# The dilated stage's first two turns and its masks made between the last products of layer 1's pairs

## What is computed

```python
def band_attend(q, k, v, d, nw):      # per residue mod d, 128-query blocks
    s = einsum('bthe,bmhe->...', q, [previous block, own block] of k)
    s = where(valid, s, NEG)          # the masks
    p = exp(s - max(s)); l = sum(p)
    return (p / l) @ v, m + log(l)

def dil_layer(x, ...):
    z = rms_norm(x, norm_g) @ w_in    # projections; norm on q and k rows
    dil_out = combine of the three groups * silu(gd)
    mem_out = mem_attend(q, mem_kv) * silu(mg)
    return x + concatenate([dil_out, mem_out]) @ w_out
```

## Time and profile before

| | us |
|---|---|
| median of three executions | 2821.64 (2819.12 to 2824.57) |
| the profiled execution, its own time | 2820.37 |
| its span | 2818.2 |
| PE busy | 2759.3 (98%) |
| DVE, ACT, POOL busy | 1758.5, 1113.7, 364.9 |
| the pairs' last product | 2286.39 to 2289.11 |
| the sample rows' matmuls ahead of it | 2284.53 to 2286.39 |
| the masks on POOL | from 2294.99, a memset of 0.44 and three selects of 0.78 together |
| the dilated stage | 2289.11 to about 2512 |

### The profile page before, as it was taken

One profiled execution on the slowest core, in us unless ns is written; L12 is line 12 of the kernel. 1 busy time (PEld: TensorE's weight loads), 2 busy tenths in 40 slices (PEclk: granted clock), 3 DMA queues, 4 the chain that ended last, 5 costly groups with the idle time before them and its releaser, 6 DMA issues.

```text
span 2818.2 us, 38685 instructions
## 1 busy us (share of the span) xinstructions
PE 2759.3 (98%) x13662; PEld 2278.4 (81%) x13662; DVE 1758.5 (62%) x3819; ACT 1113.7 (40%) x3357; POOL 364.9 (13%) x574
## 2 busy tenths in 40 slices
PE   7999999999999999999999999999999989989999
PEld 6787888888787888888787888788888779988887
DVE  5486666768678633325575767776765656557664
ACT  5433131222326224215434453532323348756532
POOL 0001010100101000000001132313324022210000
PEclk9999999999999999999999999999999999999999
DMA  4276555555676634324266676868777788647642
GB/s 169 86 239 199 190 186 175 183 181 176 199 244 205 202 106 145 99 99 150 94 250 229 224 245 226 286 219 286 262 267 246 253 283 286 215 151 244 200 142 95
DMA packets 282873, 559.16 MB, mean 198 GB/s; under 512 B 31168, under 2 KB 81920, under 8 KB 282680
## 3 DMA queue, kind: packets, MB, share of 16 engines
q1 hardware_dynamic: 248440, 453.89, 49.5%
q0 software_dynamic: 34240, 102.80, 10.0%
HBM read 423.85 MB, written 132.72 MB: 197 GB/s over the span
## 4 chain that ended last, share of the span: by engine, by line
PE 93%; DVE 3%; DMA 2%; ACT 1%; issue 1%; SPq 0%; DVEq 0%; ACTq 0%
PE ps L130 26%; PE ps L132 25%; PE ps L131 25%; PE ps L3560 2%; PE ps L3532 2%; PE ps L3081 2%; PE ps L3065 1%; PE ps L3569 1%; PE ps L3119 1%; PE ps L237 1%; PE ps L2122 1%; PE ps L2390 1%; PE ps L3548 1%; PE ps L3543 1%; DMA tok_b_dram<-shared_o 1%; PE ps L1149 1%
## 5 line engine op out<-in xcount | busy, mean ns | idle before, releaser
L130 PE MATMUL ps<-b_wp,b_sring 128*128 128x512 f32 x640 | 250.3, 391 | 4.4 <-DMA b_sring<-sums_dram 3.7
L131 PE MATMUL ps<-b_wp,b_sring 128*128 128x512 f32 x640 | 249.8, 390 | 0.0
L132 PE MATMUL ps<-b_wp,b_sring 128*128 128x512 f32 x640 | 249.7, 390 | 0.0
L130 PE MATMUL ps<-a_sring,a_wp 128*128 128x512 f32 x512 | 199.5, 390 | 2.6 <-DMA a_sring<-sums_a_dram 2.6
L132 PE MATMUL ps<-a_sring,a_wp 128*128 128x512 f32 x512 | 199.3, 389 | 0.0
L131 PE MATMUL ps<-a_sring,a_wp 128*128 128x512 f32 x512 | 199.2, 389 | 0.0
L132 PE MATMUL ps<-b_wp,b_xtlo 128*128 128x512 f32 x480 | 186.8, 389 | 0.0
L131 PE MATMUL ps<-b_wp,b_xthi 128*128 128x512 f32 x480 | 186.8, 389 | 0.0
L130 PE MATMUL ps<-b_wp,b_xthi 128*128 128x512 f32 x480 | 186.8, 389 | 0.0
L960 DVE TENSOR_TENSOR shared_o<-ps,b_spare 128x512 f32<-128x512 f32 x160 | 109.7, 685 | 100.5 <-PE ps L132 83.1
L802 ACT ACTIVATE ps<-shared_o 128x128 f32<-128x128 f32 (+1 forms) x408 | 108.0, 265 | 154.7 <-DVE shared_o L960 146.9
(11 more groups left out here) (461 smaller groups left out, 6823.5 us busy)
## 6 DMA issues: line engine op xcount, KB each, us to landing
b_sring<-sums_dram SPq DMA_DIRECT2D x160, 512.0 KB, 5.1
a_sring<-sums_a_dram SPq DMA_DIRECT2D x128, 512.0 KB, 5.0
b_raws<-w_b_dram SPq DMA_DIRECT2D x176, 256.0 KB, 4.3
a_raws<-w_a_dram SPq DMA_DIRECT2D x140, 256.0 KB, 4.4
kv_dram<-shared_o POOLq DMA_DIRECT2D x96, 256.0 KB, 4.2
tok_b_dram<-shared_o POOLq DMA_DIRECT2D x96, 256.0 KB, 4.5
front<-tok_b_dram SPq DMA_DIRECT2D x96, 256.0 KB, 3.7
front<-grp_dram SPq DMA_DIRECT2D x48, 260.0 KB, 4.3
```

The costliest lines, as they stand in the source:

```text
L130: pe.matmul(acc, a_hi, b_hi, start=first, stop=False)
L131: pe.matmul(acc, a_hi, b_lo, start=False, stop=False)
L132: return pe.matmul(acc, a_lo, b_hi, start=False, stop=last)
```

## The change

A new class `Opening` holds the stage's first tiles and its buffers, and its methods are called from both stages.

- PE turns tile 0 ahead of product `N - 4`, the memory keys ahead of `N - 3` and tile 1 ahead of `N - 2`. These turns use banks 6 and 7. ACT and DVE make their copies at the same `n`, ahead of what they do for that product.
- POOL builds the masks at `n = N - 8`, ahead of the stores that follow.
- The sample rows' matmuls in phase 6 stand ahead of the product before the last, and their finish stands ahead of the last output's, in every pair.
- DVE no longer waits for the stores. SP loads tiles 0 to 3's queries and keys and the memory keys, then the values of tile 0, waits for the last product, and loads the values of tiles 1 to 3. Behind tile 4's queries and keys it waits for the stores of all outputs, then loads values 4 and all that follows.
- ACT runs one exponential on a column of `ident` at the start of the stage. The stage's loop on PE starts with round 2.
- The buffers lie elsewhere: values in three pieces (`dil_v0`, `dil_v1`, `dil_v4`).

```diff
@@ shared_stage
+    SAMPLED = {0: TP - 3, 1: TP - 1, 5: TP - 1, 6: TP - 2}
...
-        if r == 0 and j:
-            return sample_out(j - 1, 1), 5, 2 * j - 1
+        if r == PN - 2 and j < len(pairs):
+            return sample_out(j, 1), 5, 2 * j + 1
...
@@ POOL
             for n in range(N + 2):
                 j, f, p = where(n)
+                if n == N - TP:
+                    pool.wait_ge(keys.reduced, keys.UNITS)
+                    opening.build_masks(pool)
@@ ACT
+                if n == N - 4:
+                    opening.copy_query(act, 0)
+                if n == N - 3:
+                    for m in range(MT):
+                        opening.memory_high(act, m)
+                if n == N - 2:
+                    opening.copy_query(act, 1)
+                if n and sample_at(n - 1):
+                    evict(sample_at(n - 1)[0], sample_at(n - 1)[1])
...
-                if n and sample_at(n - 1):
-                    evict(sample_at(n - 1)[0], sample_at(n - 1)[1])
@@ DVE
-                at_once = n < N and out_of(n) is not None and kinds[out_of(n)] == "copy"
+                at_once = n == N - 1 or n < N and out_of(n) is not None and kinds[out_of(n)] == "copy"
+                if n == N - 4:
+                    opening.copy_keys(dve, 0)
+                if n == N - 3:
+                    for m in range(MT):
+                        opening.memory_low(dve, m)
+                if n == N - 2:
+                    opening.copy_keys(dve, 1)
@@ PE
-                if p == (TP - 1 if f else TP - 3) and f in (0, 1, 5, 6):
+                if f in SAMPLED and p == SAMPLED[f]:
                     sample(j, f)
+                if n == N - 4:
+                    opening.turn(pe, 0)
+                if n == N - 3:
+                    opening.turn_memory(pe)
+                if n == N - 2:
+                    opening.turn(pe, 1)
                 product(n)
@@ class Opening
+    def query_bank(self, s):
+        return self.core.ps[:, 0 if s > 1 else 6, :]
+    def turn(self, pe, s):
+        u, ident = s % self.U, self.core.ident
+        pe.wait_ge(self.qk_in[u], 32 * (s // self.U + 1))
+        if s == 1:
+            pe.wait_ge(self.mem_low, MT)
+        if s:
+            pe.wait_ge(self.q_copied, s)
...
@@ dil_stage, SP
             for sem, count in tail.stored(tail.projected):
                 sp.wait_ge(sem, count)
-            sp.wait_ge(*tail.made)
+            sp.wait_ge(*tail.made(0))
             sp.wait_ge(*tail.split)
             sp.wait_ge(*tail.weights)
+            sp.wait_ge(*tail.keys)
+            opening.load(sp, 0)
+            opening.load_memory(sp)
+            for s in range(1, U):
+                opening.load(sp, s)
+            load_values(0)
+            sp.wait_ge(*tail.made(NT // 2))
+            for s in range(1, U):
+                load_values(s)
+            for s in range(U, TILES):
+                opening.load(sp, s)
+                if s == U:
                     for sem, count in tail.stored(tail.outputs[1]):
                         sp.wait_ge(sem, count)
+                load_values(s)
...
@@ dil_stage, ACT, DVE and PE
+            act.activation(front.stat[:, 0, 0:1], ident[:, 0:1], ACT.Exp)
...
-            dve.wait_ge(masked, 3)
-            for sem, count in tail.stored(tail.outputs[1]):
-                dve.wait_ge(sem, count)
+            dve.wait_ge(opening.masked, 3)
...
-            for s in range(TILES + 2):
-                if s == 0:
-                    pe.wait_ge(*tail.bank_free(0))
+            for s in range(2, TILES + 2):
                 if s == 2:
-                    pe.wait_ge(*tail.outputs)
+                    for bank in range(3):
+                        pe.wait_ge(*tail.bank_free(bank))
...
                 if s == 3:
-                    pe.wait_ge(mem_low, MT)
+                    pe.wait_ge(*tail.outputs)
```

More of the change, by code:

```diff
@@ L503, in __init__, with shared_stage @@
         self.wh1, self.wl1 = prep.buffers(stack)
-def shared_stage(core, block, lead, prep, first, pairs, ops, bufs, xt_hi, xt_lo, xs_hl, spare, w_out, keys):
+def shared_stage(core, block, stack, lead, prep, first, pairs, ops, bufs, xt_hi, xt_lo, xs_hl, spare, w_out, keys, opening):
     nc, ps, io = core.nc, core.ps, core.io
@@ L3215, in out_stage, with dil_stage @@
                     stored=lambda t: (y_out[t % 2], 16 * (t // 2 + 1)) if t < NT else (dec.y_out, 16))
-def dil_stage(core, block, tail, q_src, kv_src, dst, front, ahead, mem_kv, ops_out):
+def dil_stage(core, block, tail, opening, dst, ahead, mem_v, ops_out):
     nc, ps, ident = core.nc, core.ps, core.ident
-    U, V, R = 4, 8, 3
+    front, place, rows = opening.front, opening.place, opening.rows
+    U, V, R = opening.U, opening.V, opening.R
     GROUPS = len(DIL)
     TILES = NT * GROUPS
[L3227 to L3234, removed]
+    kv_src, dst = opening.kv_src, dst[::-1]
@@ L3343, in _ @@
         def _(pool):
-            pool.wait_ge(*tail.keys)
-            pool.memset(masks[:, :], 0.0).then_inc(zeroed, 1)
-            pool.wait_ge(zeroed, 1)
-            for at, sign in ((0, -1), (1, 1), (2, -1)):
-                cols = masks[:, at * P:(at + 1) * P]
-                pool.affine_select(out=cols, in_=cols, compare_op=ALU.is_ge, fill=NEG, base=0,
-                                   pattern=[[-sign, P]], channel_multiplier=sign).then_inc(masked, 1)
             for s in range(TILES):
@@ L3397, in _ @@
                     exps(s - 2, 1)
-                if real(s):
-                    copy_query(s)
-                if s == 2:
-                    for m in range(MT):
-                        memory_high(m)
+                if s > 2 and real(s):
+                    opening.copy_query(act, s)
             act.wait_ge(front.qturned, 1)
@@ L3504, in _ @@
                     minima(s - 2, 1)
-                if real(s):
-                    copy_keys(s)
-                if s == 2:
-                    for m in range(MT):
-                        memory_low(m)
+                if s >= 2 and real(s):
+                    opening.copy_keys(dve, s)
             next_groups_max()
@@ L3559, in sums @@
                     for i, key in enumerate(order(s)):
-                        m = pe.matmul(sums_at(s)[:, h, :], pt[:, h, i, :], v_b[:, key % V, cols], start=(i == 0),
+                        m = pe.matmul(sums_at(s)[:, h, :], pt[:, h, i, :], v_at[key % V][:, cols], start=(i == 0),
                                       stop=(i == len(order(s)) - 1))
@@ L3656, in build @@
             keys.scores(st)
+            with ExitStack() as early:
+                opening = Opening(core, early, [io["tok_b"][g][0:T, :] for g in range(len(DIL))],
+                                  [io["kv"][g][0:T, :] for g in range(len(DIL))], mem_kv(1, 0), ops)
             with ExitStack() as ws:
@@ L3677, in build @@
                          Pair(gate(4), gate(5), norm_b)]
-                tail = shared_stage(core, block, lead, prep, (key(0), value(0)), pairs, ops, bufs, xt_hi, xt_lo, xs_hl,
-                                    spare, io["w_out_b"], keys)
-            front = Front(core, st)
-            dil_stage(core, block, tail, [io["tok_b"][g][0:T, :] for g in range(len(DIL))],
-                      [io["kv"][g][0:T, :] for g in range(len(DIL))],
-                      [io["grp"][g * T:(g + 1) * T, :] for g in range(len(DIL))], front, src,
-                      (mem_kv(1, 0), mem_kv(1, 1)), ops)
+                tail = shared_stage(core, block, st, lead, prep, (key(0), value(0)), pairs, ops, bufs, xt_hi, xt_lo, xs_hl,
+                                    spare, io["w_out_b"], keys, opening)
+            front = opening.front
+            front.open(core, st)
+            core.sb(st, "front_held", [P, 10800])
+            dil_stage(core, block, tail, opening, [io["grp"][g * T:(g + 1) * T, :] for g in range(len(DIL))], src,
+                      mem_kv(1, 1), ops)
             out_stage(core, block, 1, src, io["x1"][0:T, :], io["y"][0:T, :], ops, io["x1"][T:TS, :], io["y"][T:TS, :],
```

188 lines of the change are left out of this document (109 added, 79 removed).

## The result

The changed kernel takes 2825.35 us (median of 20 runs, 2820.73 to 2828.11), the kernel before 2821.4 (20 runs, 2816.57 to 2824.57). The ratio is 1.0013, with a 95% interval of 1.0007 to 1.0019: about 3.9 us more, slower beyond doubt and still within the 0.2% that the prediction counts as no change. The forecast was +5.2. The profiled execution of the changed kernel took 2826.09 (span 2824.2), 5.7 more than that of before.

What follows compares the result with a forecast made beforehand. PE was taken to be busy nearly throughout, with waits at the dilated stage's start. A gain of 5.3 us (22.85 - 2.6 - 14.9) against 10.6 for tile 0's wait and its clock gave +5.2 us, 2826.8, range +2.5 to +8.

Steps and rivals of the forecast that it cites:

- Where the time goes: PE before tile 0's turn, ahead of the last four products: a 7.7 us wait for a load issued 1.1 us late.
- The memory keys: Landing at the latest 2287.7 to 2288.6, with PE coming to them about 2290: load hidden, no wait.
- The last product's end: End of the last product before the dilated stage: 2289.11 + 2.6 moved work + 7.7 wait + 2.9 clock = 2302.3.
- The clock's 2.9: PE at half speed behind the wait for tile 0: 2.9 us lost.
- Behind the last product: From the last product's end to tile 5's turn: 14.9 us, set by tile 5's late load, where 22.85 stood before.
- The clock there: Between last product and tile 5: waits may lower PE's clock, 1.5 us more, covered by tile 5's late load.
- The end: Whole kernel: +5.2 us, 2826.8, from tile 5's start moving from 2311.96 to 2317.2.
- the forecast's own signs of being wrong: Tile 0 coming without a wait, the clock staying at full, or the tiles behind tile 5 waiting too.
- Rival A: At tile 0's turn: the tile lands fast, wait 4.1 and clock 1.6; -0.2 us, 2821.4; chance 0.22.
- B: At tiles 5 and 6: loads pile up, tile 6 waits about 1.5 more; +8.3 us, 2829.9; chance 0.13.
- C: At tile 0's turn: PE doesn't wait, the load being issued before 2273; -5.3 us, 2816.3; chance 0.05.
- D: Nothing on the whole: a hidden stall at the other pairs' ends takes or gives a microsecond or two; chance 0.05.

Runs made afterwards that it cites:

- the filler: The changed kernel with sixty transposes of the identity, read by nobody, in front of tile 0's turn: 2821.59 us, and 2822.9 when run again.
- the tile 5 edits: Tile 5's queries and keys loaded ahead of the wait for the stores: 2815.6 us with three loads early, 2824.45 on the changed kernel alone.
- the three early loads: The changed kernel with the loads of tile 0, the memory keys and tile 1 each issued behind an earlier ring load: 2814.28 us.
- tile 0's loads early: The changed kernel with only tile 0's queries and keys loaded some 8 us earlier, memory keys and tile 1 left in place: 2820.85 us.

## Why the prediction was right, and where not

- **Where the time goes: right.** A wait of 7.7 us in front of tile 0's turn was forecast, 7.62 and 7.36 came. It comes from SP's order (keys asked for 1.02 us after PE is ready, 1.1 forecast) and from the landing (6.55; 6.6 forecast). The Trainium skill (DMA: Bandwidth & Descriptors, section "Anatomy of one DMA — SWDGE (gpsimd) path") has the fit of 2.0 us plus the bytes over 436e3, 2.6 us here as an estimate; it was measured on transfers issued in another way than SP's, and no run here has such a load alone. This one took 3.9 more, at a DMA share of 0.90 (2277 to 2284). Moving the three loads gave back 10.1 us of the 10.6 that wait and clock had in the sum.
- **The memory keys: right, for a reason worth seeing.** They waited for nothing, only because tile 0's wait stood in front: without it they waited 3.40.
- **The last product's end: 2302.3 forecast,** 2302.1 in the profile, measured as before (the last matmul starts at 2301.85, and the next could follow 0.227 us later). The clock's 2.9 had a true value of 2.8 in that profile, 1.3 in the second, and 2 to 3 by the two timings with the filler: I had one number for a term that spreads by 1.5 between executions of one kernel, and that the sum met the first profile so closely is in part luck.
- **Behind the last product: right in its steps.** 1.49 before the first scores (1.5 forecast), the last store issued 4.6 behind the product's end (4.4) and landing 4.58 later (4.2 or more), tile 5's keys issued 10.1 behind it (9.9) and landing in 4.27 (4.4), tile 5 turned at 2316.52 (2317.2). ACT's table load stands by itself, for 1.28, as said.
- **The clock there: wrong twice.** I said it might fall by the waits on the way (1.5, 1.8, 0.3 and 1.0 forecast; 1.49, 1.49 and 0.76 came), 1.5 us lost: it did not, 1.00 throughout. And I said that tile 5's wait "covers what the clock costs", and forgot the clock behind that wait: 1.69 us (tile 5 to tile 6: 4.79 against 3.10). This is the step by which the profiled execution lies at +6.27 and not near +4.6. No term of the sum stands for it.
- **The end: +5.2 forecast, +3.95 measured.** The profiled executions of the changed kernel are +6.5 and +3.4 in the stretch, and the second is like the median. The forecast was worked out for what the first shows; in the second the clock lost 1.5 us less at tile 0 and nothing at tile 5, tile 5 waited 1.11 instead of 1.92, and 0.9 came back at tile 9. With the clock at tile 0 at 1.3 in place of 2.9 the sum gives +3.6. The wait at tile 9 is one of the forecast's own signs of being wrong ("if the tiles behind tile 5 waited too"); it came, at 0.9.
- **Rival A** (the tile lands fast) fell: it landed in 6.55. **B** (loads pile up) didn't come in the first profile; what the changed kernel's second profile and the filler's first show, 0.90 and 1.27 at tile 9, is its mechanism at a small size (behind the memory's values in SP's queue), and with the tile 5 edits it eats most or all of the gain. **C** (no wait) is what the three early loads make: it was priced at -5.3, and measured -6.1. **D:** the other pairs' ends moved nothing that shows (sample rows' move alone: ratio 1.0, with an interval of 0.9991 to 1.0009, 2.5 us either way).

## What to carry to other kernels

When work is moved forward on one engine, move its loads forward in their queue too: a load has a place in the issuing engine's order, and behind an instruction that waits for a later event it can't be early. Look at every load that the moved work needs, not only at the first, since the first wait hides the next ones (tile 0's hid 3.4 us of the memory keys'). Where DMA and PE are both full behind the moved point, a wait taken away at one tile can come back at a later one (in two kernels here), so count a gain only as far as the transfers can follow, and look at which other load stands in the pile.

## What the hardware did that I had not expected

- PE stood still for 5.7 of 16 us, in waits of 1.49, 1.49, 0.76 and 1.92, with the granted clock at 1.00 until the last one; behind the 1.92 it fell to 0.57 for four us. In two other kernels waits of 1.95 (tile 0's loads early) and 1.78 (three loads early) at the same tile left it at 1.00, and behind waits of 7.62 and 7.36 in two executions of one kernel it cost 2.8 and 1.3. The length of the wait alone doesn't say whether the clock falls; what else decides was not found.
- Sixty matmuls that nobody reads, put where PE would stand still, made the changed kernel 2 to 3 us faster. Thirty that outlasted the wait by 1.5 to 2.8 us cost 1.1 to 3.7.
- Loads of 256 KB landed in 4.27 us at tile 5 (DMA share 0.76 from 2311 to 2317) and in 6.55 at tile 0 (0.90 from 2277 to 2284) in one execution, and a store of 256 KB in 3.52 in one kernel and 5.85 in another; the one that sets the time should be priced by its own row.
